# The end of a two-block program with a token a partition: the gate g2 folded into the rows, h transposed early, squares summed on ScalarE, the factors on a diagonal

## The reference

```python
def rmsnorm(x, g):
    xf = x.astype(jnp.float32)
    inv = lax.rsqrt(jnp.mean(xf * xf, axis=-1, keepdims=True) + EPS)
    return (xf * inv * g.astype(jnp.float32)).astype(x.dtype)

def second_block(x, c, ...):
    h = x
    c_act = jax.nn.silu(c)
    for l in range(DEPTH):                       # DEPTH = 1
        mod = c_act @ w_ada[l] + b_ada[l]
        sh1, sc1, g1, sh2, sc2, g2 = jnp.split(mod, N_ADA, axis=-1)
        ...                                      # SSD branch, pooling branch, gates
        mixed = (g_ssd * y_ssd + g_pool * y_pool) @ w_out[l]
        h = h + g1[:, None, :] * mixed
        u2 = modulate(rmsnorm(h, norm_ffn_g[l]), sh2, sc2)
        h = h + g2[:, None, :] * moe_ffn(u2, w_router[l], router_bias[l], we_gate[l], we_up[l], we_down[l],
                                         ws_gate[l], ws_up[l], ws_down[l])
    return rmsnorm(h, final_norm_g)

def moe_ffn(u, ...):
    ...                                          # scores, 8 experts a token, slots of 128 tokens
    def expert_block(args):
        toks, ws, e = args
        xb = u_pad[toks]
        hid = jax.nn.silu(xb @ we_gate[e]) * (xb @ we_up[e])
        return (hid @ we_down[e]) * ws[:, None]
    ...
    routed = jax.ops.segment_sum(y_slots.reshape(n_slots, D), slot_tok, num_segments=N + 1)[:N]
    shared = (jax.nn.silu(uf @ ws_gate) * (uf @ ws_up)) @ ws_down
    return (routed + shared).reshape(Bsz, S, D)
```

## Time and profile before

| | us |
|---|---|
| median of 3 runs | 2560.13 |
| lowest and highest of them | 2556.67, 2562.9 |
| the profiled execution | 2554.49 |
| its span | 2552.3 |
| from the landing of the first tile of the sums (2517.70) to the end of the span | 34.6 |

### The profile page before, as it was taken

How to read it: one execution, slowest core, us unless ns; L and a number is a source line. 1 busy time by engine, 2 the same in 40 slices (tenths; PEclk the granted TensorE clock), 3 DMA queues, 4 the chain that set the end, 5 groups by cost and what they waited for, 6 DMA issues and landing times.

```text
span 2552.3 us, 28331 instructions
## 1 busy us (share of the span) xinstructions
PE 2348.0 (92%) x10424; PEld 1505.9 (59%) x10425; DVE 1174.9 (46%) x1798; ACT 693.0 (27%) x1080; POOL 662.7 (26%) x417
## 2 busy tenths in 40 slices
PE   6999897899998999999999698999989989988996
PEld 5886343687786866677777575467433333333334
DVE  3545423668986145588888633014711111111113
ACT  3333335333323133344334232112311111101111
POOL 2331000334424332333333132022122222222220
PEclk9998668899998998999999799999989999999998
DMA  3223000235554212222222122121498789989853
GB/s 127 87 71 132 0 1 1 66 99 191 166 179 159 74 64 85 83 83 66 67 67 67 34 66 99 66 99 54 170 342 276 219 309 299 352 320 364 260 163 116
DMA packets 163725, 353.72 MB, mean 139 GB/s; under 512 B 9456, under 2 KB 100592, under 8 KB 145456
## 3 DMA queue, kind: packets, MB, share of 16 engines
q1 hardware_dynamic: 146352, 297.18, 32.7%
q0 software_dynamic: 16128, 51.06, 8.3%
q10 hardware_dynamic: 1152, 4.19, 0.4%
HBM read 326.19 MB, written 34.60 MB: 141 GB/s over the span
## 4 chain that ended last, share of the span: by engine, by line
PE 77%; DMA 9%; DVE 8%; ACT 2%; issue 2%; POOL 1%; SPq 1%; POOLq 0%; DVEq 0%; ACTq 0%
PE bank L749 25%; PE bank L1306 10%; PE bank L1046 7%; PE bank L740 7%; PE bank L1327 5%; DMA arena<-in_we_up 4%; PE bank L960 3%; PE bank L895 2%; PE bank L872 2%; DMA arena<-in_we_down 2%; PE bank L1285 2%; PE bank L758 1%; DMA arena<-in_w_up 1%; PE bank L1085 1%; PE bank L886 1%
## 5 line engine op out<-in xcount | busy, mean ns | idle before, releaser
L1306 PE MATMUL bank<-arena,hn 128*64 128x512 f32 x1536 | 347.2, 605 | 23.5 <-DMA arena<-in_we_up 22.8
L656 POOL TENSOR_TENSOR w_low_flat<-arena,in_high 128x1024 fp32r<-128x1024 f32 (+1 forms) x73 | 184.3, 2546 | 386.8 <-ACT in_high L1626 386.7
L1306 PEld LDWEIGHTS bank<-arena,hn 128*64 128x64 f32 x1536 | 117.2, 140 | 246.2 <-issue 245.1
L1327 PE MATMUL bank<-arena 128*64 128x512 f32 x768 | 175.4, 598 | 28.5 <-DVE arena L2450 27.9
L2445 DVE TENSOR_TENSOR inv<-inv,bank 128x256 f32<-128x256 f32 x48 | 20.2, 421 | 363.0 <-ACT inv L1845 363.0
L1845 ACT ACTIVATE inv<-bank 128x256 f32<-128x256 f32 x48 | 18.4, 384 | 552.2 <-PE bank L1306 552.2
L740 PE MATMUL bank<-arena 128*128 128x512 f32 x320 | 142.7, 605 | 6.4 <-DMA arena<-in_w_br_ssd 6.4
L640 POOL TENSOR_TENSOR w_low<-arena,w_high 128x2048 fp32r<-128x2048 f32 x22 | 104.4, 4744 | 160.7 <-ACT w_high L1538 160.7
L2457 DVE TENSOR_SCALAR sq<-bank,arena 128x512 f32<-128x512 f32 x96 | 72.1, 751 | 147.7 <-PE bank L1327 147.7
L749 PE MATMUL bank<-x_high,w_high 128*128 128x512 f32 x336 | 133.4, 397 | 2.6 <-POOL w_low L640 2.6
L1046 PE MATMUL bank<-in_x,in_high 128*128 128x512 f32 x336 | 135.5, 403 | 0.0
(11 more groups left out here) (437 smaller groups left out, 4912.6 us busy)
## 6 DMA issues: line engine op xcount, KB each, us to landing
arena<-in_we_gate SPq DMA_DIRECT2D x47, 1024.0 KB, 5.7
arena<-in_we_up SPq DMA_DIRECT2D x47, 1024.0 KB, 7.9
arena<-in_we_down SPq DMA_DIRECT2D x47, 1024.0 KB, 6.6
arena<-in_w_in SPq DMA_DIRECT2D x40, 1024.0 KB, 5.4
arena<-in_w_ada SPq DMA_DIRECT2D x12, 2048.0 KB, 8.0
arena<-in_w_up SPq DMA_DIRECT2D x22, 1024.0 KB, 10.7
arena<-in_w_in SPq DMA_DIRECT2D x18, 512.0 KB, 5.1
arena<-in_w_out SPq DMA_DIRECT2D x4, 2048.0 KB, 8.1
```

What stands on the lines that cost most here:

```text
L656: pool_eng.tensor_tensor(in2_tile(j, "low"), in2_tile(j, "whole"), in2_tile(j, "high").bitcast(f32), ALU.subtract).then_inc(S("w_low"), 1)
L1306: ins = nc.tensor.matmul(rows_of(out, c), columns_of(moe["xT"][:, p, :], k, c), gate_up[:, :, k, :], start=k == 0, stop=k == KD - 1)
L1327: ins = nc.tensor.matmul(rows_of(banks[5 + half], c), columns_of(moe["hidT"][:, p, :], k, c), moe["dn"][:, 2 * p + c, at:at + 512], start= ...
```

## The change

Five things are changed, all for the rows of the MoE and the end of the program.

1. The gate in rows. Behind the last product of `wo2` and ahead of `norm_sums("n5")`, PE makes eight products of 128 x 128 that put `g2` into all partitions, a feature a column, in banks 1 and 2. ACT copies them into a new tile `g2` (128 x 1024), behind the root of n5 and ahead of the shifts of n5.
2. The shared matrix. GpSimd multiplies `sdn`, the down matrix of the shared expert, by `g2` in place (two instructions of 128 x 1024), ahead of its wait for the router's product. `shared_down` waits for that. In the loop `block_out` multiplies by the slot's weight and by `g2` in one `scalar_tensor_tensor`, where it was a `tensor_scalar`. So the sums in DRAM hold g2 times the MoE's result.
3. h transposed in the wait. Behind the last block PE transposes `h` into all eight banks (32 transpositions), a token a partition. For each tile DVE then adds: bank + first sum (two instructions of 128 x 512, in place in `acc[0]`), and that + second sum (one of 128 x 1024).
4. Squares on ACT. One `Square` of 128 x 1024 with `accum_out` gives a column with the sum over the features of each token; the root takes it with scale 1/D. Ahead of it ACT takes one root of a constant, which nothing reads.
5. The factors on a diagonal. DVE takes the reciprocal and multiplies the identity by it (`LAST_INV`, 128 x 128). PE takes the products of the rows with this diagonal, 8 a tile: they transpose back to a feature a partition and apply the factor. DVE writes features 0 to 511 of the tile with the final gain (one `tensor_tensor` of 128 x 512), ACT features 512 to 1023 (four `activation` of 128 x 128 with the gain as scale). SP stores the halves by two semaphores.

The diff, with one line of context ahead of a change and eight spaces of indent taken off:

```diff
--- before.py
+++ after.py
@@ -260,7 +260,11 @@
 acc = [lay(n * TT * D, acc=(TT, D))["acc"] for n in range(2)]
-LAST_SQ = sq.rearrange("p (a b) (c n) -> p a (b c) n", a=2, n=P)
+moe.update(lay(late["end"] + 2 * KD * P, g2=(D,)))
+LAST_SUM = ROW_SUM[:, 0:TT]
+LAST_INV = sq[:, :, 0:P]
@@ -287,8 +291,8 @@
 ACT_MADE = {name: n + 1 for n, name in enumerate(("lam_exp", "fg_ln", "c_act", "expA", "dt_ln", "dtp_done",
-                                                  "tok_done", "scores", "sc_done"))}
-PE_MADE = {name: n + 1 for n, name in enumerate(("tok_ready", "sc_ready", "counted", "runs_counted",
+                                                  "tok_done", "g2_row", "scores", "sc_done"))}
+PE_MADE = {name: n + 1 for n, name in enumerate(("tok_ready", "g2_spread", "sc_ready", "counted", "runs_counted",
@@ -597,8 +601,8 @@
     for tt in range(TT):
-        for half in range(2):
-            sp.wait_ge(S("norm_out"), KD * NORM_OUT["n6"] + KD * tt + 4 * half + 4)
+        for half, (done, value) in enumerate((("norm_out", KD * NORM_OUT["n6"]), ("half_out", 0))):
+            sp.wait_ge(S(done), value + tt + 1)
@@ -662,6 +666,11 @@
+    pool_eng.wait_ge(S("shared_in"), 48)
+    pool_eng.wait_ge(S("act_made"), ACT_MADE["g2_row"])
+    for k in range(2):
+        pool_eng.tensor_tensor(moe["sdn"][:, k, :], moe["sdn"][:, k, :], moe["g2"], ALU.mult)\
+                .then_inc(S("down_gated"), 1)
@@ -1146,6 +1155,13 @@
                        5 * KD).then_inc(S("product"), 1)
+    for half in range(2):
+        pe.wait_ge(S("h_done"), 3 * KD + half + 2)
+        for i in range(4):
+            k = 5 * KD + 4 * half + i
+            ins = nc.tensor.matmul(banks[1 + half][:, i * P:(i + 1) * P], mod[:, k:k + 1].to_broadcast([P, P]), ident,
+                                   start=True, stop=True)
+    ins.then_inc(S("pe_made"), 1)
@@ -1198,6 +1214,7 @@
         pe.wait_ge(S("sh_hT"), tt + 1)
+        pe.wait_ge(S("down_gated"), 2)
@@ -1350,42 +1367,24 @@
-    def add_halves(tt):
-        pe.wait_ge(S(f"panel_in_slot{tt}"), counted[tt] + 32)
+    for n in (0, 1, 2, 3, 4, 7, 5, 6):
+        if n in (5, 6):
+            pe.wait_ge(S("y_copied"), pairs_but_one * 4 + (2 * TT + n - 2))
+        for q in range(4):
+            k = 4 * (n % 2) + q
+            ins = nc.tensor.transpose(banks[n][:, q * P:(q + 1) * P], h[:, k, n // 2 * P:(n // 2 + 1) * P], ident)
+        ins.then_inc(S("acc_T"), 1)
+    for tt in range(TT):
+        pe.wait_ge(S("norm_inv"), NORMS["n6"] + tt + 1)
         for half in range(2):
-            if tt >= 2:
-                pe.wait_ge(S("h_done"), 4 * KD + KD * (tt - 2) + 4 * half + 4)
                 d = 4 * half + q
-                for n in range(2):
-                    ins = nc.tensor.matmul(banks[2 * (tt % 2) + half][:, q * P:(q + 1) * P],
-                                           acc[n][:, tt, d * P:(d + 1) * P], ident, start=n == 0, stop=n == 1)
+                ins = nc.tensor.matmul(banks[2 * tt + half][:, q * P:(q + 1) * P], acc[0][:, tt, d * P:(d + 1) * P],
+                                       LAST_INV[:, tt, :], start=True, stop=True)
-    def last_sums(tt):
-        for k in range(KD):
-            if k % 4 == 0:
-                pe.wait_ge(S("norm_sq"), KD * NORMS["n6"] + 2 * tt + k // 4 + 1)
-            ins = nc.tensor.matmul(banks[4 + tt % 2][:, 0:1], LAST_SQ[:, tt % 2, k, :], const("ones_d")[:, 0:1],
-                                   start=k == 0, stop=k == KD - 1)
-        ins.then_inc(S("norm_sum"), 1)
-    def last_spread(tt):
-        pe.wait_ge(S("norm_inv"), NORMS["n6"] + tt + 1)
-        nc.tensor.matmul(banks[6 + tt % 2][:, 0:P], RECIP[:, tt:tt + 1].to_broadcast([P, P]), ident, start=True,
-                         stop=True).then_inc(S("last_spread"), 1)
-    for tt in range(TT):
-        add_halves(tt)
-        if tt >= 1:
-            last_sums(tt - 1)
-            last_spread(tt - 1)
-    last_sums(TT - 1)
-    last_spread(TT - 1)
@@ -1771,6 +1770,9 @@
     squares("n5", after_wo2, 2)
+    act.wait_ge(S("pe_made"), PE_MADE["g2_spread"])
+    nc.scalar.activation(moe["g2"][:, 0:512], banks[1][:, :], ACT.Copy)
+    nc.scalar.activation(moe["g2"][:, 512:D], banks[2][:, :], ACT.Copy).then_inc(S("act_made"), 1)
@@ -1856,17 +1858,27 @@
+    nc.scalar.activation(RECIP[:, 0:TT], EPS_COLUMN.to_broadcast([P, TT]), ACT.Sqrt)
+    def last_half(tt):
+        act.wait_ge(S("acc_T"), 2 * TT + 2 * tt + 2)
+        for q in range(4):
+            ins = nc.scalar.activation(hn[:, 4 + q, tt * P:(tt + 1) * P], banks[2 * tt + 1][:, q * P:(q + 1) * P],
+                                       ACT.Copy, scale=col("final_norm", 4 + q))
+        ins.then_inc(S("half_out"), 1)
     for tt in range(TT):
-        for half in range(2):
-            act.wait_ge(S("h_done"), 4 * KD + KD * tt + 4 * half + 4)
-            if tt >= 2:
-                act.wait_ge(S("norm_sum"), SUMS["n6"] + tt - 1)
-            nc.scalar.activation(LAST_SQ[:, tt % 2, 4 * half:4 * half + 4, :],
-                                 h[:, 4 * half:4 * half + 4, tt * P:(tt + 1) * P], ACT.Square)\
-              .then_inc(S("norm_sq"), 1)
-        act.wait_ge(S("norm_sum"), SUMS["n6"] + tt + 1)
-        nc.scalar.activation(RECIP[:, tt:tt + 1], banks[4 + tt % 2][:, 0:1], ACT.Sqrt, bias=EPS_COLUMN)\
+        act.wait_ge(S("h_done"), 4 * KD + tt + 1)
+        nc.scalar.activation(acc[1][:, tt, :], acc[0][:, tt, :], ACT.Square, accum_out=LAST_SUM[:, tt:tt + 1])\
+          .then_inc(S("norm_sq"), 1)
+        act.wait_ge(S("norm_sq"), KD * NORMS["n6"] + tt + 1)
+        nc.scalar.activation(RECIP[:, tt:tt + 1], LAST_SUM[:, tt:tt + 1], ACT.Sqrt, bias=EPS_COLUMN, scale=1.0 / D)\
           .then_inc(S("norm_root"), 1)
+        if tt >= 1:
+            last_half(tt - 1)
+    last_half(TT - 1)
@@ -2454,8 +2466,9 @@
             dve.wait_ge(S(("moe_y", "down_through")[half]), b + (1 + 2 * half))
-            nc.vector.tensor_scalar(moe["y"][:, p, 512 * half:512 * half + 512], banks[5 + half][:, :],
-                                    moe["wcol"][:, p:p + 1], None, ALU.mult).then_inc(S("y_copied"), 1)
+            nc.vector.scalar_tensor_tensor(moe["y"][:, p, 512 * half:512 * half + 512], banks[5 + half][:, :],
+                                           moe["wcol"][:, p:p + 1], moe["g2"][:, 512 * half:512 * half + 512],
+                                           ALU.mult, ALU.mult).then_inc(S("y_copied"), 1)
@@ -2475,37 +2488,39 @@
-        now = slice(tt * P, (tt + 1) * P)
-        for k in range(KD):
-            if k % 4 == 0:
-                dve.wait_ge(S("acc_T"), 2 * tt + k // 4 + 1)
-            nc.vector.scalar_tensor_tensor(h[:, k, now], banks[2 * (tt % 2) + k // 4][:, k % 4 * P:(k % 4 + 1) * P],
-                                           mod[:, 5 * KD + k:5 * KD + k + 1], h[:, k, now], ALU.mult, ALU.add)\
-              .then_inc(S("h_done"), 1)
+        dve.wait_ge(S("acc_T"), 2 * TT)
+        dve.wait_ge(S(f"panel_in_slot{tt}"), counted[tt] + 32)
+        for half in range(2):
+            now = acc[0][:, tt, 512 * half:512 * half + 512]
+            counted_step(nc.vector.tensor_tensor(now, banks[2 * tt + half][:, :], now, ALU.add))
+        steps_done()
+        nc.vector.tensor_tensor(acc[0][:, tt, :], acc[0][:, tt, :], acc[1][:, tt, :], ALU.add).then_inc(S("h_done"), 1)
         dve.wait_ge(S("norm_root"), NORMS["n6"] + tt + 1)
-        nc.vector.reciprocal(RECIP[:, tt:tt + 1], RECIP[:, tt:tt + 1]).then_inc(S("norm_inv"), 1)
+        step(nc.vector.reciprocal(RECIP[:, tt:tt + 1], RECIP[:, tt:tt + 1]))
+        nc.vector.tensor_scalar(LAST_INV[:, tt, :], ident, RECIP[:, tt:tt + 1], None, ALU.mult)\
+          .then_inc(S("norm_inv"), 1)
-        now = slice(tt * P, (tt + 1) * P)
-        dve.wait_ge(S("last_spread"), tt + 1)
-        for k in range(KD):
-            nc.vector.scalar_tensor_tensor(hn[:, k, now], h[:, k, now], col("final_norm", k),
-                                           banks[6 + tt % 2][:, 0:P], ALU.mult, ALU.mult)\
-              .then_inc(S("norm_out"), 1)
+        dve.wait_ge(S("acc_T"), 2 * TT + 2 * tt + 1)
+        nc.vector.tensor_tensor(hn[:, 0:4, tt * P:(tt + 1) * P], banks[2 * tt].rearrange("p (k n) -> p k n", n=P),
+                                col("final_norm", 0, 4).unsqueeze(2).to_broadcast([P, 4, P]), ALU.mult)\
+          .then_inc(S("norm_out"), 1)
+    last_h(0)
+    last_inverse(0)
     for tt in range(TT):
-        last_h(tt)
-        if tt >= 1:
-            last_inverse(tt - 1)
-            last_out(tt - 1)
-    last_inverse(TT - 1)
-    last_out(TT - 1)
+        if tt + 1 < TT:
+            last_h(tt + 1)
+        last_out(tt)
+        if tt + 1 < TT:
+            last_inverse(tt + 1)
 # ---- launch: one core; kernel() lays the inputs out ----

```

## The result

| | before, us | changed, us | ratio, 95% interval |
|---|---|---|---|
| first set (4 runs each) | 2558.65 | 2542.17 | 0.9941 [0.9922, 0.9960] |
| second set (20 and 6) | 2555.90 | 2547.59 | 0.9966 [0.9955, 0.9978] |
| third set (17 and 8) | 2554.87 | 2546.55 | 0.9963 [0.9949, 0.9977] |
| profiled execution (span) | 2554.49 (2552.3) | 2551.77 (2549.8) | |

The change makes the kernel faster, by 0.3 to 0.6%. Forecast were 6.7 us and a time of 2548 to 2560. The executions of the first set ran from 2538.39 to 2551.77, so the profiled one is the slowest of its four.

A forecast was written before the change was run, and what follows sets the result against it. At the end it took TensorE as the bound, DMA bounding the first tile alone, and a single chain behind wo2. -8.4 and +1.7 gave -6.7 us, from the median 2560.13 to 2553.4; range 2548 to 2560.

The forecast's parts named there:

- Transposing h early: Behind the last block, 32 transpositions on TensorE hidden by the wait for the sums, done 8.3 us ahead of landing: 0.
- A tile at the end: Final norm and output: a ring of DVE, ScalarE, DVE with 4.85 us a tile; end 8.4 us earlier, bounds 6.0 to 10.3.
- The gate put into rows: Norm behind wo2: eight products ahead of n5's sums of squares on a full TensorE, +1.7 us, bounds +1.6 to +2.2.
- GpSimd's products: Shared expert's down matrix times g2, two products beside DVE's norm instructions: cost 0, upper bound 5.17 us.
- the second factor in the loop: block_out multiplies by g2 as well, 0.750 us against 0.751 for the old instruction, 96 of them: 0.
- The loop: Rival: block_out's new instruction lengthens the 48 blocks; 0.14 us each erases the gain, 0.3 makes it 7.7 slower; 8%.
- a longer loop: Sign of being wrong: the loop is longer from its first gather to its last product.
- Sum: Whole kernel: -8.4 at the end plus 1.7 for the gate, -6.7 us.
- The rivals: Four alternatives: the lock 8%, a slower relay 17%, the delay swallowed 7%, the loop longer 8%.
- the lock: Rival: DVE's norm waits out GpSimd's gate products, up to 5.1 us more, so -1.6 and 2558.5 us; 8%.
- the relay: Rival at the end: hand-overs and untried forms make each tile 0.7 us slower, 2.8 in all, so -3.9, 2556.2; 17%.
- swallowed: Rival: the gate's 1.7 us vanish in the loop's waits on expert matrices, so -8.4 and 2551.7 us; 7%.

The follow-up runs named there:

- e11: The changed kernel with each tile's eight transpositions of h put behind that tile's landing; 2550.16 us, ratio 0.9974 to the kernel before.
- e3: The kernel before with only the gate's parts put in and the old end, so g2 is applied twice; 2556.50 us, ratio 1.0004.
- e2: The changed kernel with the new end alone, g2 left out and block_out a tensor_scalar again; 2548.18 us, ratio 0.9965 to the kernel before.
- e8: The kernel before plus eight unread 128 x 128 products behind the spread of n5's factors; 2554.41 us, ratio 0.9997.
- e14: The kernel before plus eight unread transpositions of h behind the loop, in the wait for the sums; 2556.96 us, ratio 1.0000.
- e4: The changed kernel with the gate's products behind n5's spread and ScalarE's copies behind the shifts; 2545.55 us, ratio 0.9962 to the kernel before.
- e6: e4 with DVE's order at the end changed, the next tile's addition ahead of a tile's reciprocal; 2540.06 us, ratio 0.9951 to the kernel before.
- e9: e6 with ScalarE's order at the end changed, tile 2's square ahead of tile 0's output; 2541.77 us, ratio 0.9948 to the kernel before.
- e7: e6 with h's transpositions made three times over and four unread products behind the first addition; 2542.10 us, ratio 0.9953 to the kernel before.
- e10: e9 with DVE's wait for both sums of a tile split into one for each sum; 2538.80 us, ratio 0.9935 to the kernel before.
- e13: The changed kernel run again without an edit, for a third trace and set of times; 2546.55 us, ratio 0.9963 to the kernel before.
- e12: The kernel before run again without an edit, for a third trace; 2552.95 us in one run.

## Why the prediction was off in size, point by point

Four stretches, in us. A: start to the last product of `wo2`; B: to the end of the router's product; C: to the first issue of the loads of the sums; D: to the end of the span.

| | A | B | C | D |
|---|---|---|---|---|
| before, three traces | 1780.1, 1779.1, 1779.9 | 16.0, 16.0, 15.9 | 716.9, 717.1, 715.6 | 39.3, 39.1, 39.6 |
| changed, three traces | 1782.8, 1774.6, 1780.0 | 17.5, 17.3, 17.3 | 719.6, 719.3, 718.1 | 30.0, 30.3, 29.8 |
| difference of the means | -0.6 | +1.4 | +2.5 | -9.3 |
| forecast of the difference | 0 | +1.7 | 0 | -8.4 |

- *Transposing h early*: right. Done 8.9 us ahead of the landing (forecast 8.3), price 0; undone, it costs 2.8 us of the end (e11).
- *A tile at the end*: mechanism right, D mis-sized: -9.3 measured against -8.4. The period was 4.49 us, not 4.85. The two additions of 128 x 512 took 1.29 and not 1.36, ScalarE's square with its reading 1.16 and not 1.30, because the reading of the accumulator starts before the square's end, and the next addition starts before the end of the diagonal. ScalarE's half of the output took 1.15 and not 1.3, a term that no row had. Against that, the last tile got TensorE at mostly half clock: 3.2 us, where the middle of 1.9 and 3.4 had been taken.
- *The gate put into rows*: right. Up to the root it is 1.6 us more (4.40 against 2.77), and B in whole grew by 1.3 to 1.5 (forecast 1.7; e3 alone 1.2). The sums of squares follow the eight products without cover, as said. In two of the three traces the spread then took 2.09 us for 8 records and not 1.17, and the router's product 8.5 and not 9.7: the clock fell at another place.
- *GpSimd's products, the second factor in the loop*: right, 0 each. The evidence for the first was thinner than it was put: of the three L2173 of the earlier trace rows only the first two ran beside GpSimd, which was done at 1166.47.
- *The loop*: put at 0 but for a rival of 8%. C was 2.5 us longer in the traces of the changed kernel, with no overlap (715.6 to 717.1 against 718.1 to 719.6). The block at 2086 us alone accounts for it: 17.8, 15.7 and 15.4 us against 19.3, 19.0 and 19.2. `block_out` is not the place: it costs what it did, and e2, which has the old one, shows 719.5. e8 and e14, the kernel before with products that nobody reads, show 719.5 and 723.9. So a sign that the prediction named for being wrong, a longer loop, showed, but C does not tell the change from any other edit, and the cause stays open.
- *Sum*: -6.7 forecast. B and D, which the change touches, give -9.3 + 1.4 = -7.9 by the traces; the two larger sets give -8.3. With C it would be -5.4, which lies just outside the intervals of both sets (gains of 5.6 and 5.9 us at their least), so the 2.5 us are not likely to be in every execution.
- *The step that failed* is the last one: "the change is counted from the median: 2560.13 - 6.7", with "the 3 us by which runs of the same kernel lie apart". Three executions stood for the level of the kernel, and the later sets put it at 2555 to 2556, 4 to 5 us lower. Of the 11.3 us between the forecast of 2553.4 and the 2542.17 of the first set, 4.7 are that level, 1.6 the size of the gain, and 4.9 the luck of four executions of the changed kernel (2547.1 in the mean of the larger sets). The prediction had a warning: its profiled execution lay 5.6 under the median. Counted from it, its 2547.8 is within 1.3 us of the two larger sets, which is luck too, since it is one execution. And the scatter was read off three numbers of one kernel. The changed kernel alone lay between 2538.39 and 2551.77. The traces show the places. Stretch A, the same code in all, had 1774.6 to 1782.8 us. About 5 of the 8 us arise between 350 and 400 us. The windows there in the second trace of the kernel before, and then in that of the changed kernel with the shortest A:

```profile
350.00:400.00 50.00, 48.06 (x126) 20.11 (x125) 16.43 (x68) 19.04 (x55) 0.00 (x0) 0.72 0.00 0
```

```profile
350.00:400.00 50.00, 47.08 (x142) 20.21 (x140) 19.26 (x80) 21.98 (x65) 0.00 (x0) 0.84 0.00 0
```

The same code, granted 0.72 in one and 0.84 in the other, and TensorE took 142 records in the window where it took 126. Stretch C scatters by another 8 us over the sixteen traces (715.6 to 723.9), in the blocks that wait for expert matrices. A runs before anything that the change touches; for C see above.
- *The rivals*: the lock did not come, the relay was faster and not slower, the new instruction in the loop made no block longer, and the 1.4 us were not swallowed, as e3 and B show.

Only in B and D is the difference clearly more than traces of the same code scatter by. A and C scatter by as much as the whole change is worth, so the profiled pair (2.7 us apart) and the first medians (16.5) stand on the two sides of 8.

## What to carry to other kernels

At the end of a program, where a few tiles pass one after the other through several engines, count the hand-overs and take out of the ring what can be done before its input lands. Then order each engine's queue so that no tile's addition or square stands behind another tile's output. A change of 8 us in 2550 is told from the stretches of a trace that it touches. Its size in the whole took more than four executions of each kernel: 20 against 6 and 17 against 8 agreed here, 4 against 4 said twice as much, and the level to count from was 4 to 5 us off with three.

## What the runs showed of the hardware

- TensorE's clock fell behind gaps as short as these: in the kernel before, 0.8 and 1.7 us around 1.2 us of work, then granted 0.50 and the router's 16 records in 9.8 us. With 1.8 us of products, useful or not, in the second gap the clock stayed at 1.00 and the 16 records took 7.0 us (e4, e6, e8, e9). In e7 and e10 the same filling products took 3.1 us themselves, mostly at the lower clock, and the router's product 7.3.
- A wait on a transfer can cost TensorE more than it lasts: 1.2 us more of it were followed by 32 records in 9.81 us in place of 7.09, granted 0.82 over the block in place of 1.00 (e13, e12).
- Eight `scalar_tensor_tensor` of 128 x 512 with one tensor in SBUF, one in PSUM and a column in SBUF took 5.36 us beside two GpSimd products of 128 x 1024, as without them.
- `activation` with a sum over the row costs 1.16 us for 128 x 1024 where a plain copy takes 1.05: of the 0.19 us of its reading about half overlaps with the square (1.06).
